# Moving the forgetting heads' gate sums and two mask additions from VectorE to GpSimd, and one exchange of memory keys later

## The reference

```python
def forgetting_attention(q, k, v, cum_logf):
    ...
        s = s + cum_logf[:, :, qs:qe, None] - cum_logf[:, :, None, :qe]
        causal = jnp.arange(qs, qe)[:, None] >= jnp.arange(qe)[None, :]
        p = jax.nn.softmax(jnp.where(causal, s, -jnp.inf), axis=-1).astype(v.dtype)
...
def chunk_band_attention(q, k, v, rel_table):
    ...
        s = jnp.einsum('bqhd,bkhd->bhqk', qc, kc, preferred_element_type=jnp.float32) * scale + bias
        valid = (start - left + jnp.arange(D_BAND)) >= 0
        p = jax.nn.softmax(jnp.where(valid, s, -jnp.inf), axis=-1).astype(v.dtype)
```

## Time and profile before

| what | value |
|---|---|
| median of 3 runs | 1869.93 us (1869.57 to 1869.94) |
| profiled execution | 1871.38 us, of which its span (first to last instruction) 1869.0 us |
| TensorE busy | 1861.5 us of the span, at full clock (1.0) throughout |
| VectorE busy | 1314.2 us |
| ScalarE busy | 1121.7 us |
| GpSimd busy | 353.6 us, nearly all of it issuing DMAs |

### The profile page before, as it was taken

How to read it: one execution, slowest core, us unless ns; L and a number is a source line. 1 busy time by engine, 2 the same in 40 slices (tenths; PEclk the granted TensorE clock), 3 DMA queues, 4 the chain that set the end, 5 groups by cost and what they waited for, 6 DMA issues and landing times.

```text
span 1869.0 us, 25371 instructions
## 1 busy us (share of the span) xinstructions
PE 1861.5 (100%) x9283; PEld 1625.0 (87%) x9283; DVE 1314.2 (70%) x1945; ACT 1121.7 (60%) x1678; POOL 353.6 (19%) x590
## 2 busy tenths in 40 slices
PE   9999999999999999999999999999999999999999
PEld 7888988888889888888888789888888888899888
DVE  6776776667777776666578986776666578877664
ACT  6776655557766655555468685655555467765552
POOL 1101223111001431122100001531122111102220
PEclk9999999999999999999999999999999999999999
DMA  9867789877568997798765566997788787658984
GB/s 304 247 186 219 223 263 303 256 233 250 166 213 242 295 281 237 217 274 255 236 182 192 160 196 204 276 279 233 227 256 252 229 259 245 214 156 234 253 257 137
DMA packets 289659, 436.43 MB, mean 234 GB/s; under 512 B 25532, under 2 KB 170144, under 8 KB 289280
## 3 DMA queue, kind: packets, MB, share of 16 engines
q1 hardware_dynamic: 260240, 352.41, 61.4%
q0 software_dynamic: 28832, 82.07, 16.2%
q10 hardware_dynamic: 464, 0.34, 0.1%
HBM read 396.43 MB, written 38.29 MB: 233 GB/s over the span
## 4 chain that ended last, share of the span: by engine, by line
PE 96%; DVE 2%; DMA 1%; ACT 0%; issue 0%; SPq 0%; ACTq 0%
PE M L1044 30%; PE M L1046 30%; PE M L1045 30%; DVE WL L1605 1%; DMA RAW<-in_w_in 1%; PE AUX L1088 1%; PE AUX L1102 0%; PE AUX L1216 0%; PE AUX L1259 0%; PE AUX L1286 0%; PE AUX L1287 0%; PE AUX L1260 0%; PE AUX L1261 0%; PE AUX L1288 0%; PE AUX L1208 0%
## 5 line engine op out<-in xcount | busy, mean ns | idle before, releaser
L1605 DVE TENSOR_TENSOR WL<-RAW,WH 128x1024 fp32r<-128x1024 f32 (+1 forms) x670 | 811.6, 1216 | 390.6 <-ACT WH L1319 387.9
L1319 ACT ACTIVATE WH<-RAW 128x1024 fp32r<-128x1024 f32 (+1 forms) x670 | 705.8, 1056 | 522.7 <-PE M L1046 468.3
L1044 PE MATMUL M<-WH,Bh 128*128 128x512 f32 (+1 forms) x1822 | 692.3, 380 | 1.1 <-DVE WL L1605 0.5
L1045 PE MATMUL M<-WL,Bh 128*128 128x512 f32 (+1 forms) x1822 | 683.9, 375 | 0.0
L1046 PE MATMUL M<-WH,Bl 128*128 128x512 f32 (+1 forms) x1822 | 683.9, 375 | 0.0
L1044 PEld LDWEIGHTS M<-WH,Bh 128*128 128x128 f32 x1822 | 344.6, 189 | 50.6 <-issue 3.5
L1046 PEld LDWEIGHTS M<-WH,Bl 128*128 128x128 f32 x1822 | 344.5, 189 | 47.1
L1045 PEld LDWEIGHTS M<-WL,Bh 128*128 128x128 f32 x1822 | 344.7, 189 | 44.8
L1357 ACT ACTIVATE AS<-M,KEEP 128x256 f32<-128x256 f32 x132 | 55.4, 470 | 76.3 <-PE M L1046 74.8
L1044 PE MATMUL M<-WH,MTh 128*128 128x512 f32 x128 | 51.0, 398 | 0.0
L1045 PE MATMUL M<-WL,MTh 128*128 128x512 f32 x128 | 48.5, 379 | 0.0
(11 more groups left out here) (533 smaller groups left out, 2859.6 us busy)
## 6 DMA issues: line engine op xcount, KB each, us to landing
RAW<-in_ffn_w_in SPq DMA_DIRECT2D x352, 256.0 KB, 4.1
RAW<-in_w_in SPq DMA_DIRECT2D x103, 512.0 KB, 4.7
RAW<-in_w_gate_up SPq DMA_DIRECT2D x176, 256.0 KB, 4.5
RAW<-in_ffn_w_out SPq DMA_DIRECT2D x88, 512.0 KB, 4.6
RAW<-in_w_down SPq DMA_DIRECT2D x44, 512.0 KB, 5.0
RAW<-in_x_w_kv SPq DMA_DIRECT2D x32, 512.0 KB, 4.2
RAW<-in_even_w_in SPq DMA_DIRECT2D x24, 512.0 KB, 4.6
RAW<-in_odd_w_in SPq DMA_DIRECT2D x24, 512.0 KB, 4.9
```

The source lines that it names most:

```text
L1044: e.matmul(out, s.hi, wh, start=s.at0, stop=False)
L1045: e.matmul(out, s.hi, wl, start=False, stop=False)
L1319: e.activation(p.WH[:, h, 0:s.size], p.RAW[:, i, 0:s.size], ACT.Copy).then_inc(k.w_hi, 1)
L1605: e.tensor_tensor(p.WL[:, h, 0:s.size], p.RAW[:, s.u % NRAW, 0:s.size], hi.bitcast(F32), ALU.subtract).then_inc(k.w_lo, 1)
```

## The change

1. The eight forgetting heads use the fused instruction that the other heads use. It takes one tile, so that tile must hold the row's gate sum as well: GpSimd adds it to `NB`, head by head, with two instructions each, 128 x 128 and 128 x 256 (new step `nctown`, eight of them).
2. GpSimd instead of VectorE adds the masks to `NB` (`nctma`) and `H` (`hmask`), two instructions of 128 x 1024 each. `nctma` stands behind the eight `nctown`. The first forgetting head on VectorE waits for `nb_masked`, the first odd head for `h_masked`.
3. The squares of `kx11` are made 3.5 places later (12 to 15.5) and taken up 1.5 places later (26 to 27.5).

```diff
@@ -29,7 +29,7 @@
     "bq": (3.2, 3.5, 9.8, 9.8), "bk": (3.2, 3.8, 10.4, 9.2), "aq": (5.7, 7.5, 10.6, 14.1), "ak": (3.2, 3.8, 6.8, 7.2),
     "dq": (3.2, 3.8, 7, 20.4), "dk": (3.2, 3.8, 7, 21), "xq00": (2.6, 3.8, 5.8, 6.8), "xq01": (3.2, 3.8, 4.6, 5.6),
     "xq10": (2, 2.6, 5.2, 6.2), "xq11": (3.2, 3.8, 6.7, 6.8), "kx00": (7.9, 8.5, 12, 26), "kx01": (8.2, 10.6, 13.8, 27.8),
-    "kx10": (5.7, 7.6, 11.4, 26), "kx11": (6.7, 8.8, 12, 26), "cu": (1, 2, 8, 8.5, 24), "df_s": (4.1, 8.2, 13.5, 18.5),
+    "kx10": (5.7, 7.6, 11.4, 26), "kx11": (6.7, 8.8, 15.5, 27.5), "cu": (1, 2, 8, 8.5, 18, 1.5, 31), "df_s": (4.1, 8.2, 13.5, 18.5),
     "df_late": (1.5, 0.6, -0.6, -0.1), "df_p": (3.1, 3.4, 3.4, 3.4), "df_pt": (5.9, 6.8, 6.2, 6.8), "df_o": (7.4, 9, 10.5, 8.3),
     "bo": (28, 28.5, 29.2, 30.1, 34.4, 36.7), "hg_s": (1.3, 6.6, 11.6, 16.3), "hg_late": (1.3, 1.3, 1.9, 2.5),
     "hg_p": (3, 5.4, 4.2, 5.4, 4.2, 5.4, 4.2, 6.6), "hg_pt": (5.6, 6.8, 5.6, 6.2, 5, 7.4, 6.5, 7.4), "hg_o": (7.6, 8.2),
@@ -712,7 +712,6 @@
             ss = []
             for hh in range(2):
                 s = self.add("hg_s", b)
-                s.turns_sign = which == "od"
                 s.late = PLACES[f"{which}_late"][hp] * hh
                 s.h, s.mate = 2 * hp + hh, ss[0] if hh else None
                 s.q, s.k = (x[64 * hh:64 * hh + 64, hp, :] for x in (Q, K))
@@ -756,7 +755,10 @@
         ct.l, ct.lf, ct.CT, ct.NCT = cl, c1.lf, S["CT"], S["NCT"]
         ld = self.add("nctld", c.end + PLACES["cu"][3])
         ld.ct, ld.rows, ld.NB = ct, S["NCT"], S["NB"]
-        ma = self.add("nctma", c.end + PLACES["cu"][4])
+        for h in range(8):
+            own = self.add("nctown", c.end + PLACES["cu"][4] + PLACES["cu"][5] * h)
+            own.NB, own.CT, own.h = S["NB"], S["CT"], h
+        ma = self.add("nctma", c.end + PLACES["cu"][6])
         ma.NB = S["NB"]
         c = self.chunk("bk", B, 0, KD, lab)
         self.head_qk(c, nm, 8, "bk", ("plain", cols(KB), 1.0, 1))
@@ -769,7 +771,6 @@
             ss = []
             for j in range(2):
                 s = self.add("df_s", b)
-                s.turns_sign = True
                 s.late = PLACES["df_late"][h] * j
                 s.mate = ss[0] if j else None
                 s.q, s.k = (x[64 * j:64 * j + 64, h, :] for x in (QB, KB))
@@ -971,7 +972,8 @@
         self.d_x = [[sem(f"d_x{t}{j}") for j in range(4)] for t in range(T)]
         self.warm_set, self.tile_done = sem("warm_set"), sem("tile_done")
         self.d_mem = [[sem(f"d_mem{l}{n}") for n in range(T)] for l in range(2)]
-        self.d_nct, self.d_nb = sem("d_nct"), sem("d_nb")
+        self.d_nct, self.d_nb, self.nb_own = sem("d_nct"), sem("d_nb"), sem("nb_own")
+        self.nb_masked, self.h_masked = sem("nb_masked"), sem("h_masked")
         self.blocked, self.hx_hi, self.hx_lo = sem("blocked"), sem("hx_hi"), sem("hx_lo")
         self.tx_made, self.d_tab1, self.d_tab2 = sem("tx_made"), sem("d_tab1"), sem("d_tab2")
         self.d_hb, self.d_hx = ([sem(f"{x}{i}") for i in range(PARKED)] for x in ("d_hb", "d_hx"))
@@ -1518,9 +1520,8 @@
             vacant(e, k, s.e)
             x = p.TMP[s.e.i]
             e.wait_ge(k.row_max, s.m_n)
-            sign = -1.0 if s.turns_sign else 1.0
-            e.activation(x[:, 0:128], aux[:, 0:128], ACT.Exp, bias=s.m[:, 0:1], scale=sign, accum_out=s.sm[:, 0:1])
-            e.activation(x[:, 128:384], aux[:, 128:384], ACT.Exp, bias=s.m[:, 1:2], scale=sign, accum_out=s.sm[:, 1:2]).then_inc(k.aux_out[b], 1)
+            e.activation(x[:, 0:128], aux[:, 0:128], ACT.Exp, bias=s.m[:, 0:1], scale=-1.0, accum_out=s.sm[:, 0:1])
+            e.activation(x[:, 128:384], aux[:, 128:384], ACT.Exp, bias=s.m[:, 1:2], scale=-1.0, accum_out=s.sm[:, 1:2]).then_inc(k.aux_out[b], 1)
         elif s.kind == "cx_s":
             if table != "l":
                 table = "l"
@@ -1867,23 +1868,14 @@
             e.wait_ge(k.aux_full[b], s.use)
             if s.kind == "df_s" and s.n == 1:
                 e.wait_ge(k.d_c2, 16)
-            if s.turns_sign:
-                own, both = (p.CHUNK, p.OPEN_CHUNK) if s.kind == "df_s" else (s.extra[:, s.h, 0:P], s.extra[:, s.h, P:3 * P])
-                e.tensor_tensor_reduce(aux[:, 0:128], aux[:, 0:128], own, -1.0, FAR, ALU.add, ALU.min, s.m[:, 0:1])
-                e.tensor_tensor_reduce(aux[:, 128:384], aux[:, 128:384], both, -1.0, FAR, ALU.add, ALU.min,
-                                       s.m[:, 1:2]).then_inc(k.row_max, 1)
-            else:
-                if s.n == 1:
-                    e.wait_ge(k.aux_out[p.ct.bank], p.ct.use)
-                ct = [p.CT[:, 8 * t + s.h:8 * t + s.h + 1] for t in range(T)]
-                e.scalar_tensor_tensor(out=aux[:, 0:128], in0=aux[:, 0:128], scalar=ct[0], in1=s.extra[:, s.h, 0:P],
-                                       op0=ALU.add, op1=ALU.add)
-                e.scalar_tensor_tensor(out=aux[:, 128:384], in0=aux[:, 128:384], scalar=ct[1], in1=s.extra[:, s.h, P:3 * P],
-                                       op0=ALU.add, op1=ALU.add).then_inc(k.dve_chain, 1)
-                chain += 1
-                e.wait_ge(k.dve_chain, chain)
-                e.tensor_reduce(s.m[:, 0:1], aux[:, 0:128], AX.X, ALU.max, negate=True)
-                e.tensor_reduce(s.m[:, 1:2], aux[:, 128:384], AX.X, ALU.max, negate=True).then_inc(k.row_max, 1)
+            if s.kind == "hg_s" and s.n == 1:
+                e.wait_ge(k.nb_masked, 2)
+            elif s.kind == "hg_s" and s.n == 9:
+                e.wait_ge(k.h_masked, 2)
+            own, both = (p.CHUNK, p.OPEN_CHUNK) if s.kind == "df_s" else (s.extra[:, s.h, 0:P], s.extra[:, s.h, P:3 * P])
+            e.tensor_tensor_reduce(aux[:, 0:128], aux[:, 0:128], own, -1.0, FAR, ALU.add, ALU.min, s.m[:, 0:1])
+            e.tensor_tensor_reduce(aux[:, 128:384], aux[:, 128:384], both, -1.0, FAR, ALU.add, ALU.min,
+                                   s.m[:, 1:2]).then_inc(k.row_max, 1)
         elif s.kind == "cx_s":
             e.wait_ge(k.aux_full[b], s.use)
             e.tensor_reduce(s.m, aux[:, :].rearrange("p (t c) -> p t c", t=2), AX.X, ALU.max, negate=True).then_inc(k.row_max, 1)
@@ -2001,15 +1993,6 @@
             e.tensor_copy(p.TB[0:8, 0:127], p.TB[0:8, 127:128].to_broadcast([8, 127])).then_inc(k.su_tab, 1)
         elif s.kind == "su_done":
             e.wait_ge(k.d_tabx, 16)
-        elif s.kind in ("nctma", "hmask"):
-            x, mask = (s.NB, p.CAUSAL) if s.kind == "nctma" else (p.H, p.CHUNK)
-            e.wait_ge(*((k.d_nb, 32) if s.kind == "nctma" else (k.d_h, 48)))
-            e.wait_ge(k.d_c2, 16)
-            for i in (0, 2):
-                v = x[:, :, i * P:(i + 1) * P]
-                e.tensor_tensor(v, v, mask.unsqueeze(1).to_broadcast([P, 8, P]), ALU.add).then_inc(k.dve_chain, 1)
-                chain += 1
-            e.wait_ge(k.dve_chain, chain)
 
 
 def gpsimd(e, k):
@@ -2112,6 +2095,23 @@
             x = p.parked_nct
             e.dma_start(s.NB[:, :, 0:P], bass.AP(x.tensor, x.offset, [[0, P], [256, 8], [1, P]])).then_inc(k.d_nb, 16)
             e.dma_start(s.NB[:, :, P:3 * P], bass.AP(x.tensor, x.offset, [[0, P], [256, 8], [1, 256]])).then_inc(k.d_nb, 16)
+        elif s.kind in ("nctma", "hmask"):
+            if s.kind == "nctma":
+                x, mask, made = s.NB, p.CAUSAL, k.nb_masked
+                e.wait_ge(k.nb_own, 8)
+            else:
+                x, mask, made = p.H, p.CHUNK, k.h_masked
+                e.wait_ge(k.d_h, 48)
+            e.wait_ge(k.d_c2, 16)
+            for i in (0, 2):
+                v = x[:, :, i * P:(i + 1) * P]
+                e.tensor_tensor(v, v, mask.unsqueeze(1).to_broadcast([P, 8, P]), ALU.add).then_inc(made, 1)
+        elif s.kind == "nctown":
+            if s.h == 0:
+                e.wait_ge(k.d_nb, 32)
+            own, both = s.NB[:, s.h, 0:P], s.NB[:, s.h, P:3 * P]
+            e.tensor_scalar(own, own, s.CT[:, s.h:s.h + 1], None, ALU.add)
+            e.tensor_scalar(both, both, s.CT[:, 8 + s.h:9 + s.h], None, ALU.add).then_inc(k.nb_own, 1)
 
 
 def x_piece(e, k, t, j):
```

## The result

The changed kernel took 1872.92 us in the median of 20 runs (1869.27 to 1876.77); the kernel before, run beside it, 1869.72 us (20 runs, 1869.43 to 1870.97). The ratio is 1.0015, 95% interval 1.0009 to 1.0021. The forecast was 1868.7 us with a range up to 1871.0: the time lies 1.9 us above the range, and 3.2 us above the time before where 1.2 us less were expected. It is inside the 0.2% that the text calls no change, but with the wrong sign. The profiled execution took 1871.19 us, its span 1869.3 us.

What follows compares the result with a forecast made beforehand. TensorE, busy 1861.5 of 1869.0 us, was taken to bound the kernel. Winning 0.81 us at 1064 and 0.42 at 1615 made 1.23 less than 1869.93, so 1868.7 us; range 1867.8 to 1871.0.

Steps and rivals of the forecast that it cites:

- 0.81 + 0.42 = 1.23 us less: Sum over two TensorE waits, before 1064 and 1615 us: both shortened, giving 1868.7 us on the median's scale.
- forecast: Main case: both waits of TensorE shortened, 1.23 us less, 1868.7 us; chance 0.68.
- GpSimd's new work: Additions and masks for NB, masks for H: estimated 22.0 and 3.9 us, costing nothing as long as the cover holds.
- both gates: VectorE's waits for GpSimd at the first forgetting head (1025.11) and first odd head (1557.27); masks expected done before.
- given back by collisions: Rival: GpSimd's additions hold up VectorE on SBUF, ScalarE waits for kx11's keys; 1869.3 to 1871.0 us, chance 0.13.
- ScalarE's wait for kx11: At the keys' taking-up near 1632.4 us: 0 to 1.2 us of ScalarE waiting for the fetches; counted as nothing.
- Fused heads, 0.81 us: Eight forgetting heads, 0.72 us less each on VectorE: TensorE's whole 0.81 us wait before 1064 us goes.
- Later squares, 0.42 us: Queries' first products, 1615 us: kx11's squares leave the low parts' way, winning 0 to 0.47 us, taken as 0.42.
- given back at the next low parts: Near 1618 us, low parts behind kx11's moved squares: 0 to 0.2 us could be lost; counted as nothing.
- The fetch of kx11 and the norm's root: Later fetch on GpSimd delays the cross attention's root, about 3.5 us later, ending 1626.7 to 1627.9, just in time.

Runs made afterwards that it cites:

- kx10_sq_early: The changed kernel with kx10's squares transposed one instruction earlier on VectorE (11.4 to 10.9); 1868.61 us, before 1870.41, ratio 0.999.
- even_kx11: The changed kernel with H's masks back on VectorE, kx11 at its new places; 1868.90 us, before 1870.41.
- write_late: even_kx11 with three fills of one column on GpSimd ahead of kx10's write, as a delay; 1873.36 us, before 1870.52.
- after_again: The changed kernel unaltered, run again beside write_late; 1873.01 us, before 1870.52, ratio 1.0013.
- even_only: The kernel before with only the fused heads and NB's additions and masks on GpSimd; 1868.92 us, before 1870.01.
- kx11_only: The kernel before with only kx11's squares and taking-up moved; 1869.84 us, before 1870.01.
- hmask_kx11: The kernel before with only H's masks on GpSimd and kx11 moved; 1870.45 us, before 1870.41.
- hmask_split: The changed kernel with each of H's two masks made as two instructions of four heads; 1869.36 us, before 1870.41.
- best: The changed kernel with kx10's squares one instruction earlier on VectorE and kx10 taken up behind two activations on ScalarE; 1868.80 us, before 1870.52.
- kx10_late: The changed kernel with kx10 taken up 1.3 places later on ScalarE, behind two activations; 1869.22 us, before 1870.01.
- kx11_back: The changed kernel with kx11's squares and taking-up at their old places; 1869.80 us, before 1870.01.

## Why the prediction was wrong

**Which step failed.** The sum "0.81 + 0.42 = 1.23 us less" holds only terms of what the change touches, and the case "forecast" took for granted that no new wait comes. The term that failed is GpSimd's new work, "Cost: nothing, as long as this cover holds": the cover held at both gates, and still the new instructions made GpSimd issue the write of kx10 0.28 us later, which together with the moved squares cost TensorE 2.72 us. Behind the moved squares the text looked at GpSimd and ScalarE for kx11 alone. It never read the row of kx10 at 1617.22, in the middle of the stretch: ScalarE already idle for 0.25 us, with the next activations behind it. Across the profiles TensorE's wait is ScalarE's idle time there less some 1 us (3.76 to 2.72, 3.77 to 2.73, 3.72 to 2.68, 2.03 to 1.16, and none up to 0.79): less than 1 us was left, and the exchange took up to 3.5 us more. The rival "given back by collisions" had the right sign but the wrong place: it priced GpSimd against VectorE on SBUF and ScalarE's wait for kx11, not the landing of kx10's write, and stopped at 1871.0. The trace of before had a warning elsewhere: at 442.25 us a write of 512 KB left 0.83 us after its transposition and 0.30 us ahead of a load, and landed after 7.1 us:

```profile
squares<-TG POOLq DMA_DIRECT2D x1, 512.0 KB, 7.1
```

**What the pieces are.** Without the wait the change takes 1.8 us (kx10_sq_early, 1868.61) or 1.5 us (even_kx11, 1868.90) less than the kernel before beside it, where 1.23 were forecast; that the two times lie near the forecast of 1868.7 is in part luck, as before took 1870.41 us beside them and not 1869.72. 1868.6 + 2.7 = 1871.3 us, a rough sum, is where five of the 20 runs lie (1871.16 to 1871.41, the profiled one among them); one lies below, at 1869.27. So the wait stands for what these five lost; the median, 1872.92, lies 1.6 us above them. Above that, the mean granted clock of a run is 0.998 or 0.999 in six of the ten above 1873 us, and 1.000 in all below; 0.001 of 1870 us is 1.9 us, about the 1.7 that write_late's windows show. In after_again all six runs from 1873.01 us up have 0.999. That the clock of each of them fell behind this wait isn't shown, since only one such execution was profiled, and four runs of 1873.31 to 1874.77 us have 1.000. So of the 3.2 us, the 1.6 us beyond the wait are explained in part only.

**Point by point.** *Fused heads, 0.81 us:* the right wait, and somewhat more than that; 0.59 us between two heads, the wait gone, and even_only 1.1 us below before, a hint. In the ten profiles with the fused heads TensorE gains 1.0 to 1.2 us between 1040 and 1064: 0.3 of them come at 1043 us already, where the text saw no wait. In the kernel before, the transposition that follows the product at 1043.95 us starts 0.96 us after it; in the changed kernel, where that product is at 1042.59 us, 0.66 us. That the fused heads alone do it, and not NB's masks, which left VectorE with them, wasn't separated. *GpSimd's work:* estimated at 22.0 and 3.9 us, measured 984.60 to 1006.65 = 22.05 and 4.72 us, and both gates were met. The parts differ from the estimate: most additions take 0.59 and 0.92 us, and four of 16 some 1 us more.

```profile
L2113 POOL TENSOR_SCALAR NB<-NB,CT x8: 594/661/1589, 984.6 to 999.2; 128x128 f32<-128x128 f32 x8
L2114 POOL TENSOR_SCALAR NB<-NB,CT x8: 912/917/1970, 985.6 to 1000.0; 128x256 f32<-128x256 f32 x8
L2108 POOL TENSOR_TENSOR NB<-NB,C x2: 2362/2860/3357, 1001.0 to 1003.3; 128x1024 f32<-128x1024 f32 x2
```

Those (ns, min/median/max) are GpSimd's lines at NB; a mask alone takes 2.36 to 2.39 us (the estimate of 2.25 us that the prediction gave by the Trainium skill, GPSIMD Engine Reference, section "Elementwise — side-by-side cycle accounting", is 5% short of these rows). VectorE's low parts of weights in the same 22 us pay too, one of seven by 1.6 us:

```profile
L1606 DVE TENSOR_TENSOR WL<-RAW,WH x7: 1216/1224/2810, 983.9 to 1004.9; 128x1024 fp32r<-128x1024 f32 x7
```

By the Trainium skill (SBUF — State Buffer, section "Who interferes with whom") a VectorE instruction with two inputs in SBUF contends with a GpSimd instruction that reads SBUF, and the ports that they share are an exclusive lock; these rows agree, on both sides now. It cost nothing, as TensorE was busy 39.00 of 39 us there. *Later squares, 0.42 us:* not realised in the changed kernel, where another input was last, as the text had allowed: VectorE stood 1.12 us until 1610.67 for ScalarE's high part of a weight, and did its low part ahead of the activations'. In the ten profiles with kx11 moved the loss was 0 to 0.12 us five times (kx11_only, hmask_kx11, hmask_split, kx10_sq_early, best) and 0.47 to 0.70 five times (the changed kernel twice, even_kx11, kx10_late, write_late): a term that comes and goes: VectorE stood 0.6 to 0.8 us for ScalarE's high part ahead of it in the first five, and 1.1 to 1.3 us in the others. What was given back at the next low parts was 0 to 0.14 us, within the 0 to 0.2 stated. *The fetch of kx11 and the norm's root:* the root was forecast some 3.5 us later; it came at 1624.11, 0.9 us later in the clock of the trace and 3.5 later when the lead of 2.6 us is taken off. That is luck: the fetch was through at 1623.23, and the root waited 0.88 us more for VectorE, which TensorE's wait had made late. In kx11_only, without that wait, the root does stand right behind the fetch, at 1624.51, and is 1.3 us later than before (1.7 without its own lead of 0.4 us) and not 3.5: the write landed sooner than the text had assumed (the fetch began 4.1 us after the write's issue, in before 6.8). Queries (1628.12) and keys (1632.95) were taken up without a wait of TensorE behind them.

**What stays open.** First, why GpSimd needs 0.83 in place of 0.55 us for one write. In the seven profiles with 0.83 or more (the changed kernel twice, kx11_back, kx10_late, kx10_sq_early, best, write_late) one packet of a DMA queue of the kind "instruction" falls 0.6 to 1.2 us after the issue; in the other seven none falls within 2 us of it. That speaks for the fetch of GpSimd's own instructions, but the packet comes behind the issue, and no run here separates it.

Second, why a write that is issued some 0.3 us later starts 2 us later. The experiments show that it does for kx10's write, not that the load behind it is the cause: what VectorE does beside the write shifts by the same time. By the Trainium skill (DMA: Bandwidth & Descriptors, section "Queues, rings and completion order") each DMA engine takes turns between its queues, a packet at a time. The trace shows another thing here, a later start: in the window shown above the write has no packet at all. Nor is shown why a lead of some 0.3 us gave a write of 5.76 us in one profile, 6.20 in another and 7.2 in three. And kx10's 4.5 us are not what a lead of 0.58 us gives elsewhere: in the kernel before, kx11's write of 512 KB (1612.80) was as far ahead of a load (1613.38) and took longer:

```profile
squares<-SQO POOLq DMA_DIRECT2D x1, 512.0 KB, 6.3
```

Third, in kx11_back and after_again TensorE also lost 0.9 and 0.7 us near 1571 (line 1218, for VectorE's division); what is behind that wait is open.

## What to carry to other kernels

Before a change that makes an engine earlier, list the waits of all in-order queues in that stretch, also those of work the change doesn't touch: a queue that already stands for 0.25 us at a transfer, with urgent work behind it, has little to give. Where work stands behind a transfer, look at what moves the transfer's issue, even by 0.3 us, and make it earlier by moving what it waits for; or take its result up behind the urgent work, which helped here (kx10_late) although the transfer stayed slow. And try a version that moves the suspect by one instruction before giving up a change: here that turned 3.2 us above before into 1.8 below.

## What the runs showed of the hardware

kx10's write of 512 KB, issued 0.58 to 0.64 us ahead of a load of 512 KB, landed after 4.43 to 4.52 us in eight profiles; issued 0.21 to 0.31 us ahead, after 5.76 to 7.25 us in five. (The one profile with 0.93 us had 5.16.) At 442 us all fourteen profiles have a write of 512 KB issued 0.29 to 0.30 us ahead of a load: it landed after 5.6 to 7.3 us. The other way round there is no rule: writes of 512 KB that were 0.5 to 0.66 us ahead took 4.4 to 9.7 us in these profiles. A wait of 2.7 us of TensorE was followed by 4 us at a granted clock of 0.54 to 0.60 in one profile, and by none in two. And the issue of kx10's write on GpSimd came 0.28 us later with 20 instructions more ahead of it in the program, and not with 2, 18 or 22.
